# mLSTM sample state update: ScalarE scales the loaded state in place and VectorE adds the outer product, in place of an outer product buffer

## What is computed

```
C_new = a_end * C + outer(k * decay, v)     # per sample row and head, 512 x 512
num   = q @ C_new                           # what the token reads from the new state
```

## Time and profile before

| | before |
|---|---|
| time, median of 3 runs | 1238.18 us (1237.99 to 1239.83) |
| profiled execution, span from the first to the last instruction | 1234.2 us |
| median less span | 4.0 us |
| PE busy | 1126.7 us, 91% of the span |
| DVE busy | 576.2 us, 47% |
| ACT busy | 304.1 us, 25% |
| mean granted clock of PE | 0.966 of full |

### The profile page before, as it was taken

The page is one execution under the profiler, slowest core; times in us unless marked ns, Lnnn a source line. Parts: engine busy times, 40 slices in busy tenths (PEclk is TensorE's granted clock), DMA queues, the critical chain, the costliest instruction groups (busy, mean ns, idle before and its releaser), DMA issues. The chain is left out here.

```text
span 1234.2 us, 14118 instructions
## 1 busy us (share of the span) xinstructions
PE 1126.7 (91%) x4725; PEld 665.1 (54%) x4725; DVE 576.2 (47%) x992; ACT 304.1 (25%) x601; POOL 102.3 (8%) x140
## 2 busy tenths in 40 slices
PE   4999999999689659999959999999999999996998
PEld 2444444444334428777745458544864476343776
DVE  1444555335647535555324454445533553466332
ACT  1121222212200001111223322442144205432310
POOL 1011111011100000000021011101110101010000
PEclk9999999999889879999979999999999999998999
DMA  8113332122257643444453992299519951894211
GB/s 231 48 41 83 86 85 68 44 58 85 88 206 255 208 163 64 138 139 138 174 164 101 330 330 88 70 329 348 118 35 304 352 135 37 286 334 153 80 69 70
DMA packets 138937, 189.22 MB, mean 153 GB/s; under 512 B 27683, under 2 KB 80531, under 8 KB 137319
## 3 DMA queue, kind: packets, MB, share of 16 engines
q1 hardware_dynamic: 111814, 156.21, 38.7%
q0 software_dynamic: 5808, 24.35, 6.3%
q10 hardware_dynamic: 21264, 8.02, 2.5%
HBM read 133.47 MB, written 55.21 MB: 153 GB/s over the span
## 5 line engine op out<-in xcount | busy, mean ns | idle before, releaser
L474 PE MATMUL pj<-w_in,hT 128*128 128x512 f32 (+1 forms) x640 | 243.6, 599 | 5.2 <-DMA w_in<-in_a_w_in 4.4
L474 PEld LDWEIGHTS pj<-w_in,hT 128*128 128x128 f32 (+1 forms) x640 | 99.2, 172 | 124.0 <-issue 123.5
L1638 DVE SCALAR_TENSOR_TENSOR state<-state,s_all,outer 128x1024 f32<-128x1024 f32 x64 | 81.2, 1283 | 99.0 <-DMA state<-in_state_C 67.5
L1827 PE MATMUL tok_ps<-w_og,hT 128*128 128x512 f32 (+1 forms) x320 | 121.5, 598 | 0.0
L1150 PE MATMUL xm_ps<-hT,shared 128*128 128x260 f32 x512 | 119.1, 392 | 1.5 <-PEq L100 1.2
L1150 PEld LDWEIGHTS xm_ps<-hT,shared 128*128 128x128 f32 x512 | 98.1, 194 | 22.6 <-issue 5.5
L1498 ACT ACTIVATE outer<-v_bcast,k_cols 128x512 f32<-128x512 f32 x128 | 81.8, 710 | 87.3 <-DMA v_bcast<-keep_v_rows 87.3
L1761 PE MATMUL col_ps<-hT,shared 128*128 128x260 f32 x384 | 86.7, 384 | 0.0
L1827 PEld LDWEIGHTS tok_ps<-w_og,hT 128*128 128x128 f32 (+1 forms) x320 | 48.7, 169 | 70.1 <-issue 64.6
L1761 PEld LDWEIGHTS col_ps<-hT,shared 128*128 128x128 f32 x384 | 72.0, 190 | 13.2 <-issue 2.6
L288 ACT COPY raw<-pj 128x512 f32<-128x512 f32 (+1 forms) x40 | 23.4, 584 | 187.6 <-PE pj L474 146.3
(11 more groups left out here) (260 smaller groups left out, 1411.7 us busy)
## 6 DMA issues: line engine op xcount, KB each, us to landing
state<-in_state_C SPq DMA_DIRECT2D x64, 512.0 KB, 5.3
out_C_sample<-state SPq DMA_DIRECT2D x64, 512.0 KB, 6.3
w_in<-in_a_w_in SPq DMA_DIRECT2D x32, 512.0 KB, 6.8
shared<-in_m_w_in SPq DMA_DIRECT2D x10, 1024.0 KB, 5.7
kv_cache<-in_cache_k SPq DMA_DIRECT2D x16, 512.0 KB, 4.6
kv_cache<-in_cache_v SPq DMA_DIRECT2D x16, 512.0 KB, 5.6
w_og<-in_m_w_in POOLq DMA_DIRECT2D x4, 2048.0 KB, 12.0
v_bcast<-keep_v_rows SPq DMA_DIRECT2D x32, 256.0 KB, 6.0
```

What stands on the lines that cost most here:

```text
L474: last = nc.tensor.matmul(pj[out, (TT * j + t) % 2, :], hT[:, k, t * P:t * P + p], w[:, j, k, :, :].rearrange("p m d -> p (m d)"), start=( ...
L1638: nc.vector.scalar_tensor_tensor(out=state[:, k % 4], in0=state[:, k % 4], scalar=s_all[:, 0, ds(h, 1), b], in1=outer[:, g], op0=ALU.mult, ...
L1827: last = nc.tensor.matmul(tok_ps[out, u % 2, :], c.hT[:, k, t * P:t * P + p], wg[:, k, :], start=(k < sums), stop=(k >= KT - sums))
```

## The change

ACT no longer makes an outer product. It multiplies the piece itself by `a_end`, in place, one instruction of 128 x 1024 for each piece (`age`, semaphore `aged`), and for that it waits for the piece's load. DVE then adds `v` times the key column to the piece, in two instructions of 128 x 512, one for each block of 128 rows, and it waits for the row v (`vb`) and for ACT. The buffer `outer` is gone.

```diff
-        outer = m.sb("outer", [P, 2, 2, M_DIM])
...
-            def outer_of(h, b):
-
-                if b == 0:
-                    act.wait_ge(kq_ready, h + 1)
-                act.wait_ge(vb_in[b % 2], 16 * (4 * h + b // 2 + 1))
+            def age(h, b):
+
                 for g in range(2):
-                    need(act, new_ready, PIECES * h + 2 * b + g - 1)
-                    for d in range(2):
-                        last = nc.scalar.activation(outer[:, g, d, :], vb[:, b % 2, :], ACT.Copy,
-                                                    scale=kc[:, 2 * g + d, b:b + 1])
-                    last.then_inc(outer_ready, 1)
+                    k = 2 * b + g
+                    need_apart(act, st_in[k % 4], 16 * (4 * h + k // 4 + 1), act_tick)
+                    nc.scalar.activation(state[:, k % 4], state[:, k % 4], ACT.Copy,
+                                         scale=s_all[:, 0, ds(h, 1), b]).then_inc(aged, 1)
...
                 for b in range(TT):
-                    outer_of(h, b)
+                    age(h, b)
                     out_gate(h, (0, NT, 1, 2, 3)[b])
-                outer_of(h, 5)
-                outer_of(h, 6)
+                age(h, 5)
+                age(h, 6)
                 prompt_state(h, 0)
-                outer_of(h, 7)
+                age(h, 7)
                 for d in range(1, FH):
                     prompt_state(h, d)
...
             def new_state(h, b):
                 for g in range(2):
                     k = 2 * b + g
-                    dve.wait_ge(outer_ready, PIECES * h + k + 1)
-                    dve.wait_ge(st_in[k % 4], 16 * (4 * h + k // 4 + 1))
-                    nc.vector.scalar_tensor_tensor(out=state[:, k % 4], in0=state[:, k % 4],
-                                                   scalar=s_all[:, 0, ds(h, 1), b], in1=outer[:, g],
-                                                   op0=ALU.mult, op1=ALU.add).then_inc(new_ready, 1)
+                    if b == 0:
+                        dve.wait_ge(kq_ready, h + 1)
+                    if g == 0:
+                        dve.wait_ge(vb_in[b % 2], 16 * (4 * h + b // 2 + 1))
+                    dve.wait_ge(aged, PIECES * h + k + 1)
+                    for d in range(2):
+                        last = nc.vector.scalar_tensor_tensor(out=state[:, k % 4, d, :], in0=vb[:, b % 2, :],
+                                                              scalar=kc[:, 2 * g + d, b:b + 1], in1=state[:, k % 4, d, :],
+                                                              op0=ALU.mult, op1=ALU.add)
+                    last.then_inc(new_ready, 1)
```

More of the change, by code:

```diff
@@ L1288, in build_mlstm @@
          toks_dve, fac_ready, diag_ready, blk_ready, skip_ready, consts, cols_exp, kq_ready, v_kept,
-         outer_ready, new_ready, sn_used, sn_taken, n_done, n_taken, n_stored, nrow_ready, nrow_used, ns_stored, ln_var,
-         ln_rstd, ln_done, chained, pool_tick, dve_tick, pe_tick) = (m.sem(n + "_d") for n in (
+         aged, new_ready, sn_used, sn_taken, n_done, n_taken, n_stored, nrow_ready, nrow_used, ns_stored, ln_var,
+         ln_rstd, ln_done, chained, pool_tick, dve_tick, pe_tick, act_tick) = (m.sem(n + "_d") for n in (
              "z_used", "og_summed", "og_tanh", "og_in", "xc_in", "xm_in", "bm_in", "n_in", "pre_in", "cols_done", "cols_act", "cols_dve",
              "z_tanh", "toks_done", "toks_act", "toks_dve", "fac_ready", "diag_ready", "blk_ready",
-             "skip_ready", "consts", "cols_exp", "kq_ready", "v_kept", "outer_ready", "new_ready", "sn_used",
+             "skip_ready", "consts", "cols_exp", "kq_ready", "v_kept", "aged", "new_ready", "sn_used",
              "sn_taken", "n_done", "n_taken", "n_stored", "nrow_ready", "nrow_used", "ns_stored", "ln_var", "ln_rstd",
-             "ln_done", "chained", "pool_tick", "dve_tick", "pe_tick"))
+             "ln_done", "chained", "pool_tick", "dve_tick", "pe_tick", "act_tick"))
         taken = {"act": toks_act, "dve": toks_dve}
```

## The result

The changed kernel takes 1256.7 us (median of 4 runs, 1254.8 to 1287.61) against 1238.1 us before (4 runs): 1.0134 times as long, interval 1.0115 to 1.0153, which is 16.6 us (14.2 to 18.9). The run of 1287.61 us was disturbed by a lower clock and is not in the ratio; the median of the other three is 1256.0 us, 17.9 us above before. The profiled execution took 1255.98 us with a span of 1254.3 us, 20.1 us more than the span of before.

A forecast was written before the change was run, and what follows sets the result against it. PE, busy for 91% of the span, was taken as the bound, so a delay counts where PE waits. 5.0 (piece 11) + 8.1 (`c_out` stalls) + 3.4 (clock) = 16.5 us on 1238.2 gave 1254.7 us, range 1243 to 1261.

The forecast's parts named there:

- Term A: At piece 11 in each head, load to ready takes 1.25 us longer and delays PE's `prompt_state` 0: 5.0 us.
- The sign that the prediction named: `prompt_state` 0 in every head waits about 1.4 us for `norm_h` 2 or for piece 11.
- The stall before `prompt_state` 3: In heads 1 and 2 PE waits for ACT's `c_out` d = 1 copy, queued behind scaling piece 15: 8.1 us.
- in head 0 ... no stall: Before `prompt_state` 3 in head 0, the copy is done at 727.1, before PE comes at 727.26 + 1.25.
- the stall in head 0 too: Rival: load 15 of head 0 may land as late as in head 1, adding about 5.6 us: 1260.3 us; chance 0.13.
- + 0.7: Load 15 in heads 1 and 2 taken to land 0.7 us later, half of some 1.3 us.
- The clock, 3.4 us: PE's clock falls to the 1.2 GHz level behind the stalls in heads 1 and 2, 1.7 us each: 3.4 us.
- The gain of the work removed: ACT's 128 outer products of 0.71 us go; gain put at nothing, at least 0, at most 2.8 us.
- faster: Rival: load 11 lands earlier without the outer-product wait, giving at most PE's 2.8 us of waiting: 1235.4 us; chance 0.05.
- The sum, 16.5 us: Whole kernel: 5.0 + 8.1 + 3.4 = 16.5 us, added to the median 1238.2 for 1254.7 us.

The follow-up runs named there:

- its control: Kernel before with `xm_head` loaded later and piece 11 used later (sample row 5 after `prompt_state` 0, `norm_h` 2 and 3 ahead of piece 11): 1236.4 us, 0.9967.

## Why the prediction was right

**Term A, 5.0 us:** 4.65 us in the trace, 5.1 and 4.7 us in the experiments. Its parts held: ACT's scaling 1.145 us (1.1 taken; the Trainium skill's estimate, ScalarE: Activation LUTs, section "What ACT_TABLE_LOAD costs", of 1.13 us agrees), DVE's pair 1.42 us (1.38 taken). The new multiply-add takes 748 ns at 128x512 over all its instructions, more than the 691 ns of the row that stood for it. The way from landing to `prompt_state` 0 grew by 1.32 us in each head, 5.3 us in all; what is missing from that is that piece 11 landed 0.1 to 0.4 us earlier in heads 0, 2 and 3 (0.1 later in head 1), counted from `sample_q` b = 0. The sign that the prediction named, about 1.4 us of waiting in every head, did not show: PE waited 1.30 us for the piece in head 1 and 0.37 in head 3, as slow products of `values` brought it late.

**The stall before `prompt_state` 3, 8.1 us:** 7.97 us, and the mechanism, its place and the bank are as predicted; the copy moved ahead takes it away. The size is right by two errors that cancel, which is luck. The step "in head 0 ... no stall" failed: there the load was issued at 721.17, 0.81 us behind `xm_head` (720.36), and ACT had the piece 8.85 us later (730.02), not 5.4. POOL, SP and ACT in head 0 of the changed kernel:

```profile
720.36 0.60 POOL L1391 DMA_DIRECT2D xm_head<-keep_xm_keep  x1
...
721.17 0.41 SPq L1328 DMA_DIRECT2D state<-in_state_C  x1
...
730.02 1.15 ACT L1494 ACTIVATE state<-state,s_all 128x1024 f32<-128x1024 f32 x1 [6.34 <-DMA state<-in_state_C]
```

That is the rival "the stall in head 0 too". And the step by which load 15 lands in heads 1 and 2 at its old time "+ 0.7" was too late. In head 1 it landed 863.88 - 857.77 = 6.1 us later in a head that itself began 6.5 us later, so 0.4 us earlier, and the stalls there are 2.5 and 2.9 us, not 3.9 and 4.2. The Trainium skill, DMA: Bandwidth & Descriptors, section "Anatomy of one DMA — SWDGE (gpsimd) path", gives its fit for transfers that GpSimd issues. Carried over to load 15, which SP issues, it makes an estimate of 3.2 us, by which no head would have stalled; the 8.4 to 8.9 us of these three loads decide against that here.

**The clock, 3.4 us:** 4.70 us, because there were three falls, of 1.4 to 1.7 us each (1.7 taken). The prediction reckoned with stalls of about 4 us in two heads; they were 2.35 to 2.75 us in three, and a fall came behind each of them. Its price was read from products of `values` that had slowed with no stall ahead of them, at a granted clock of 0.62 from 955.5 to 960 in the kernel before, and was near enough for these.

**The gain of the work removed, nothing:** right as far as it can be told. With the need of piece 11 moved, the changed kernel and its control differ by 0.8 us, less than these times tell apart. The rival "faster" did not come true in any form; ACT's 10 us less are idle time.

**The sum, 16.5 us:** 16.6 us by the ratio, 17.3 by the rows, 17.9 by the medians.

## What to carry to other kernels

A step that makes an in-order engine wait for a load is priced by what stands behind it in that engine's program, not by its arithmetic: list the copies that free another engine's banks and put them ahead of the wait. Where a chain of load, update and use has no slack, each further engine in it adds its full duration once per round, and the cure here was to move the use; moving `w_og`, which competes with the load, put it ahead of other loads that PE needs. And a stall of a few microseconds on TensorE can bring slower products behind it, and is to be priced with them.

## What the runs showed that was not expected

How long PE stands does not alone decide whether its clock falls. In the kernel with the copy first, PE waited for piece 11 2.21 us in head 1, 2.22 us in head 2 and 1.97 us in head 3. PE's timeline shows `prompt_state` 0 behind these waits:

```profile
842.46 1.05 PE L1816 MATMUL sn_ps<-state,q_mask 128*32 128x512 f32 x4 [2.21 <-DVE state L1638]
843.71 3.70 PE L1858 MATMUL tok_ps<-v_m,shared 128*128 128x512 f32 x8 [0.20 <-DVE og L1663]
...
971.30 1.85 PE L1816 MATMUL sn_ps<-state,q_mask 128*32 128x512 f32 x4 [2.22 <-DVE state L1638]
973.08 4.56 PE L1858 MATMUL tok_ps<-v_m,shared 128*128 128x512 f32 x8
...
1102.40 4.75 PE L1858 MATMUL tok_ps<-v_m,shared 128*128 128x512 f32 x8
```

The granted clock was 1.00 from 842.46 to 847.40, 0.73 from 971.30 to 977.60 and 0.74 from 1100.50 to 1107.10. Waits of nearly the same length left the products behind them at full speed once and slowed them twice. In the changed kernel with `w_og` late the shorter of two waits was followed by slow products and the longer by fast ones (heads 1 and 2):

```profile
867.44 5.40 PE L1856 MATMUL tok_ps<-v_m,shared 128*128 128x512 f32 x8 [1.11 <-ACT c_out L1473]
...
1004.45 3.70 PE L1856 MATMUL tok_ps<-v_m,shared 128*128 128x512 f32 x8 [1.22 <-ACT c_out L1473]
```

And the clock fell at `values` with no wait ahead, in four heads of the changed kernel and in two of the kernel before. What decides is left open.

DVE multiplies a piece of 128x1024 by one number a partition in 757 ns, where ACT takes 1145 ns, and where its own multiply-add of two tensors takes 748 ns for half as many numbers. The Trainium skill, VectorE: DVE Perf Modes, section "Mode 2×_2P — use both read ports for one tensor", has 32-bit operations on a single tensor in SBUF at twice the rate of those on two; these rows agree. With the scaling on DVE the whole update takes 2.2 us a piece on one engine, and from landing to ready 0.4 us less than over ACT and DVE.
